# A hybrid decoder layer on one core: the first quarter of x and the first half slab by pairs of blocks

## The chip, the cores and the metric

One core of a Trainium2 chip runs the whole layer as one program. The metric is the time of one execution on the device in microseconds (us). Five engines work side by side: TensorE (PE, matmuls and transposes; its weight loads are shown as PEld), VectorE (DVE), ScalarE (ACT), GpSimd (POOL) and SyncE (SP, which here does little but issue DMAs). They meet only at semaphores.

## The reference

The layer takes x (256 tokens by 2048 features, float32) and one wide input projection, whose result is split over a state-space branch, latent attention and two gates; then an output projection, a layer norm, a SwiGLU feed-forward part and a second layer norm. Only the start of the input projection matters here:

```python
z = h @ w_in[l]                     # h = x (256, 2048)
u_ssm, c_q, c_kv, k_rope_raw, gate_logits = jnp.split(z, split_at, axis=-1)
```

## The kernel before, in words

All matmuls contract over features. A float32 operand is split in two parts that TensorE takes at full speed: a high part (a copy rounded by ScalarE) and a low part (VectorE: the value less its high part). A product of two blocks is then three matmuls: high by high, high by low, low by high.

**Weights** are packed on the host into slabs of 128 partitions by 1024 columns (8 blocks of 128 by 128, 512 KB). SP loads them into a ring of four buffers `raw`; ScalarE writes `whi` from them, VectorE `wlo`, TensorE multiplies. A load waits for the semaphore `lo_dve`, which counts finished low parts, since then its buffer is free. The first slabs (index `FRONT0 + n`) come in halves of 512 columns (`load_part`, `half_high`, `half_low`, `half_part`), so that work can begin sooner.

**x** is needed with features on the partitions. SP loads it in quarters of 512 columns, each as two loads for the two halves of the tokens (`load_x(q)`, semaphores `in_x[2q + t]`) into `xrow`. TensorE turns it by 128 by 128 transposes into PSUM (`turn_x`), one bank to a pair k of blocks (256 features): 4 transposes to a pair. ScalarE copies a bank's high part to `xT` (`x_high(k)`), VectorE its low part (`x_low(k)`).

**Order.** Everything is written by hand, one list for each engine, and each engine runs its own list in order. At the start SP issues two loads of x and two half slabs, and ScalarE itself issues the first half slab of the first slab (`load_part(ac, 0, 0)`), on a queue of its own. TensorE multiplies a zeroed tile eight times (`warm(8)`), waits for x, turns pairs 0 and 1 for each half of the tokens, multiplies the zeroed tile once more (`warm(1)`), and runs `first_part`: 12 matmuls of the first half slab by the first quarter of x (4 high by high, 4 of `wlo`, 4 by the low part of x), then `half_part(1, 0, 1)`, 12 more, then the turns of the next quarter. Each matmul there (a "product" below) has 256 columns.

The functions that the change touches, and what calls them, as the profile numbers them:

Of the kernel before, what the change touches and what calls it, by code (L numbers as in the profile page):

```python
# [21 lines left out]
P = 128  # L22
TOK = 256
# [22 lines left out]
FRONT0, FRONT_PER, FRONT_TURNS = 2, 4, 9  # L46
# [40 lines left out]
F32 = mybir.dt.float32  # L87
F32R = mybir.dt.float32r
I32 = mybir.dt.int32
ALU = mybir.AluOpType  # L90
ACT = mybir.ActivationFunctionType
# [39 lines left out]
def build(nc, slabs, x, pos, consts, cols, ssm, ssm_b, ssm_c, ln_rows, out):  # L131
    with ExitStack() as ctx:
        def sem(name):
            return ctx.enter_context(nc.semaphore(name))
# [17 lines left out]
        raw = at("raw", o, [P, RING, SLAB]); o += RING * SLAB * 4  # L152
        whi_at = o
        whi = at("whi", o, [P, RING, SLAB], F32R); o += RING * SLAB * 4
        wlo = at("wlo", o, [P, RING, SLAB], F32R); o += RING * SLAB * 4
# [35 lines left out]
        xrow = at("xrow", o, [P, 2, D]); o += 16384  # L191
# [10 lines left out]
        turn = at("turn", o, [P, 2, TOK])  # L202
# [45 lines left out]
        ps = ctx.enter_context(nc.psum_tensor("ps", [P, 8, 512], F32))  # L248
# [6 lines left out]
        ident = cst[:, C_ID:C_ID + P]  # L255
# [2 lines left out]
        raw_ready = [sem(f"raw_ready{s}") for s in range(RING)]  # L258
        hi_ready, lo_dve, slab_used = sem("hi_ready"), sem("lo_dve"), sem("slab_used")
        half_raw = [sem(f"half_raw{n}") for n in range(4)]  # L260
        half_hi, half_lo = sem("half_hi"), sem("half_lo")
        early_ready = [sem(f"early_ready{n}") for n in range(EARLY)]
        early_hi, early_lo, early_used = sem("early_hi"), sem("early_lo"), sem("early_used")
        h_shift, normed_act = sem("h_shift"), sem("normed_act")
# [3 lines left out]
        in_x = [sem(f"in_x{n}") for n in range(8)]  # L268
# [3 lines left out]
        xt_psum, xt_hi, xt_lo = sem("xt_psum"), sem("xt_hi"), sem("xt_lo")  # L272
# [53 lines left out]
        def load_part(eng, n, h):  # L326

            s, cut = (FRONT0 + n) % RING, slice(h * 512, h * 512 + 512)
            eng.dma_start(raw[:, s:s + 1, cut], slabs[FRONT_ORDER[n]:FRONT_ORDER[n] + 1, :, cut].rearrange("a p n -> p a n")
                          ).then_inc(half_raw[n] if h == 0 else raw_ready[s], 16)  # L330
# [5 lines left out]
        def _(sy):  # L336
# [15 lines left out]
            x_v = x.rearrange("(t p) d -> p t d", p=P)  # L352

            def load_x(q):
                for t in range(2):
                    sy.dma_start(xrow[:, t, q * 512:q * 512 + 512], x_v[:, t, q * 512:q * 512 + 512]
                                 ).then_inc(in_x[2 * q + t], 16)

            def load_half(n, h):
                load_part(sy, n, h)  # L360

            def front_load(v):
                load(FRONT_ORDER[v - FRONT0] if v < FRONT0 + 8 else v - FRONT0, v % RING, lo_dve, v - (RING - 1))
            load_x(0)
            load_half(1, 0)
            load_half(2, 0)
            load_x(1)
# [178 lines left out]
        def _(ac):  # L546
# [15 lines left out]
                nc.scalar.activation(whi[:, s, :], raw[:, s, :], ACT.Copy).then_inc(hi_ready, 1 + empty)  # L562


            load_part(ac, 0, 0)

            def x_high(k):
                ac.wait_ge(xt_psum, k + 1)
                nc.scalar.activation(xT[:, 2 * k:2 * k + 2, 0, :],
                                     ps[:, 2 + k % 5, :].rearrange("p (a t) -> p a t", a=2), ACT.Copy).then_inc(xt_hi, 1)  # L570

            def half_high(n, h):
                s, cut = (FRONT0 + n) % RING, slice(h * 512, h * 512 + 512)
                if h == 0:
                    ac.wait_ge(half_raw[n], 16)
                else:
                    ac.wait_ge(raw_ready[s], 16 if s >= FRONT0 else 32)
                nc.scalar.activation(whi[:, s, cut], raw[:, s, cut], ACT.Copy).then_inc(
                    half_hi if h == 0 else hi_ready, 1 + FRONT0 if (n, h) == (0, 1) else 1)

            half_high(0, 0)
            x_high(0)
            x_high(1)
            half_high(1, 0)
            half_high(2, 0)
# [333 lines left out]
            for k in range(4):  # L919
                high(0, DOWN0, 4, k + RING)  # L920
                half, cut = slice(64 * (k // 2), 64 * (k // 2) + 64), slice(1024 * (k % 2), 1024 * (k % 2) + 1024)
# [33 lines left out]
        def _(pe):  # L955
# [37 lines left out]
            def warm(n):  # L993

                for _ in range(n):
                    mm(ps[:, 1, 0:P], prob[:, 0:P], prob[:, 0:P], start=True, stop=True)

            def turn_x(q):
                for t in range(2):
                    pe.wait_ge(in_x[2 * q + t], 16)  # L1000
                    for k in (2 * q, 2 * q + 1):
                        if k >= 5:

                            pe.wait_ge(xt_lo, k - 4)
                        for a in range(2):
                            kt = 2 * k + a
                            ins = nc.tensor.transpose(ps[:, 2 + k % 5, a * TOK + t * P:a * TOK + (t + 1) * P],
                                                      xrow[:, t, kt * P:(kt + 1) * P], ident)
                        if t == 1:
                            ins.then_inc(xt_psum, 1)  # L1010

            def blocks(bank, w, s, b, kt0, n, a, first=False, last=False):

                for m in range(n):
                    ins = mm(ps[:, bank, 0:TOK], w[:, s, (b + m) * P:(b + m + 1) * P], xT[:, kt0 + m, a, :],  # L1015
                             start=(first and m == 0), stop=(last and m == n - 1))
                return ins

            def first_part():

                pe.wait_ge(half_hi, 1)
                for k in range(2):
                    pe.wait_ge(xt_hi, k + 1)
                    blocks(0, whi, FRONT0, 2 * k, 2 * k, 2, 0, first=(k == 0))
                pe.wait_ge(half_lo, 1)
                blocks(0, wlo, FRONT0, 0, 0, 4, 0)
                for k in range(2):
                    pe.wait_ge(xt_lo, k + 1)
                    blocks(0, whi, FRONT0, 2 * k, 2 * k, 2, 1)

            def half_part(n, h, bank):

                s, kt = (FRONT0 + n) % RING, 4 * h + (8 if n == 3 else 0)
                if h == 0:
                    pe.wait_ge(half_hi, n + 1)
                else:
                    pe.wait_ge(hi_ready, FRONT0 + n + 1)
                for k in range(2):
                    pe.wait_ge(xt_lo, kt // 2 + k + 1)
                    blocks(bank, whi, s, 4 * h + 2 * k, kt + 2 * k, 2, 0, first=(n < 3 and h == 0 and k == 0))  # L1040
                    blocks(bank, whi, s, 4 * h + 2 * k, kt + 2 * k, 2, 1)
                if h == 0:
                    pe.wait_ge(half_lo, n + 1)
                else:
                    pe.wait_ge(lo_dve, FRONT0 + n + 1)
                ins = blocks(bank, wlo, s, 4 * h, kt, 4, 0, last=(n == 3 and h == 1))
                if h == 1:
                    ins.then_inc(slab_used, 1 + FRONT0 if n == 0 else 1)
# [19 lines left out]
                    front_half(i, e, 1)  # L1068

            pe.wait_ge(warm_ready, 1)  # L1070
            warm(8)
            pe.wait_ge(ident_ready, 1)
            turn_x(0)
            warm(1)
            first_part()
            half_part(1, 0, 1)
            turn_x(1)
            half_part(2, 0, THIRD)
# [29 lines left out]
            for i in range(HG):  # L1108
# [182 lines left out]
                for h in range(2):  # L1291
                    head_low(i, 6 + h)
                    for t in range(2):
                        ins = row_tile(TP + t, (6 + h) % RING, t, cT, range(CT + 2 * h, CT + 2 * h + 2), h == 0, h == 1)
# [18 lines left out]
            for half in (0, 1):  # L1313
                for e in range(2):
# [3 lines left out]
                    for n in ((0, 1, 2, 3, 4, 5), (6, 7))[half]:  # L1318

                        pe.wait_ge(y_lo, n + 1)  # L1320
                        ins = fold_tile(e, e, n, yT, (n,), n == 0, n == UT - 1)
# [52 lines left out]
            for k in range(RING):  # L1374
                late_low(OUT0 + 24 + k)
                for t in range(2):
                    if k == 0:
                        row_bank(6 + t)
                    ins = out_part(k, t, first=(k == 0))
                ins.then_inc(slab_used, 1)  # L1380
            for k in range(RING, OUT_PER):
                late_low(OUT0 + 24 + k)
                ins = out_part(k, 0, last=(k == OUT_PER - 1))
# [3 lines left out]
            for k in (6, 7):  # L1387
                ins = out_part(k, 1, c1=256, last=(k == 7))
# [34 lines left out]
            for k in range(KT):  # L1423
# [8 lines left out]
                else:  # L1432
                    for e in range(2):
                        ins = early_block(k, e)
# [90 lines left out]
        def _(ve):  # L1525
            st = Steps(ve, dve_step)
            V = nc.vector
# [5 lines left out]
            def x_low(k):  # L1533
                ve.wait_ge(xt_hi, k + 1)
                V.tensor_tensor(xT[:, 2 * k:2 * k + 2, 1, :], ps[:, 2 + k % 5, :].rearrange("p (a t) -> p a t", a=2),
                                xT[:, 2 * k:2 * k + 2, 0, :].bitcast(F32), ALU.subtract).then_inc(xt_lo, 1)

            def half_low(n, h):
                s, cut = (FRONT0 + n) % RING, slice(h * 512, h * 512 + 512)
                if h == 0:  # L1540
                    ve.wait_ge(half_hi, n + 1)
                else:
                    ve.wait_ge(hi_ready, FRONT0 + n + 1)
                V.tensor_tensor(wlo[:, s, cut], raw[:, s, cut], whi[:, s, cut].bitcast(F32), ALU.subtract
                                ).then_inc(half_lo if h == 0 else lo_dve, 1 + FRONT0 if (n, h) == (0, 1) else 1)

            ve.wait_ge(index_ready, 1)
            V.tensor_scalar(ident, index[:], 0.0, None, ALU.is_equal).then_inc(ident_ready, 1)
            half_low(0, 0)
            x_low(0)  # L1550
            x_low(1)
            half_low(1, 0)
            half_low(2, 0)
# [808 lines left out]
```

## Time and profile before

| What | us |
|---|---|
| time, median of 3 runs (1322.74 to 1323.9) | 1323.16 |
| time of the profiled execution | 1323.33 |
| its span, from the first to the last instruction | 1321.3 |
| busy: TensorE | 1313.5 |
| busy: VectorE | 844.5 |
| busy: ScalarE | 650.8 |
| TensorE waiting ahead of its first product | 1.9 |

Times in the profile count from the span's start. A group of instructions in the timeline has its start, its length, the engine, the line in the program, the operation and the tiles it writes and reads, with xN for N records; a record is one pass of TensorE, and a matmul of two float32 tiles takes two. "Idle before" is the time in which the engine stood still ahead of it, with what ended that. A DMA's time to landing runs from its issue to its semaphore.

### The profile page before, as it was taken

The page shows a single profiled execution, that of the slowest core. Times are in us where ns is not written, and L with a number is a line of the kernel's source. Part 1 is how long each engine was busy: PE and PEld are TensorE (multiplying, and loading weights), DVE is VectorE, ACT ScalarE, POOL GpSimd, SP SyncE. Part 2 cuts the span into 40 slices and gives each one's busy share as a digit, 9 for nine tenths or more (in the row PEclk, how much of TensorE's full clock was granted, in tenths as well). Part 3 has the DMA queues.
Part 4 walks back from the last instruction along what each step waited for, and adds up shares of the span by engine and source line. Part 5 has one row for each costly group of instructions (what it writes and reads, how often), then busy time and mean ns, then how long its engine had stood idle before and what let it go on. Part 6 is the DMA issues. An engine that isn't in the chain of part 4 may idle for free.

```text
span 1321.3 us, 28135 instructions
## 1 busy us (share of the span) xinstructions
PE 1313.5 (99%) x10970; PEld 1241.9 (94%) x10970; DVE 844.5 (64%) x1263; ACT 650.8 (49%) x931; POOL 23.4 (2%) x52
## 2 busy tenths in 40 slices
PE   9999999999999999999999999999999999999998
PEld 9999999999999998889999999999999998888887
DVE  5887978787796776587565555555555546545545
ACT  5666557474656554365444444444444453334332
POOL 0022000000010000000000000000000000000000
PEclk9999999999999999999999999999999999999999
DMA  8666554554466776745666666666666676666572
GB/s 288 208 204 181 165 169 145 160 161 161 148 182 213 238 239 204 253 148 162 193 195 194 194 190 192 191 193 196 194 194 190 206 240 193 196 183 207 173 212 110
DMA packets 80782, 253.14 MB, mean 192 GB/s; under 512 B 16656, under 2 KB 17616, under 8 KB 80592
## 3 DMA queue, kind: packets, MB, share of 16 engines
q1 hardware_dynamic: 79024, 250.97, 60.2%
q8 instruction: 47, 0.77, 0.3%
q0 software_dynamic: 1408, 0.63, 0.2%
q10 hardware_dynamic: 288, 0.66, 0.1%
q14 instruction: 15, 0.12, 0.0%
HBM read 248.01 MB, written 2.10 MB: 189 GB/s over the span
## 4 chain that ended last, share of the span: by engine, by line
PE 95%; DVE 2%; DMA 2%; ACT 1%; issue 0%; SPq 0%; ACTq 0%; DVEq 0%
PE ps L975 21%; PE ps L977 21%; PE ps L976 21%; PE ps L987 9%; PE ps L988 9%; PE ps L989 9%; DMA raw<-slabs 1%; PE ps L1216 1%; DVE wlo L516 1%; PE ps L1015 1%; ACT whi L562 1%; PE ps L1212 1%; PE ps L1157 0%; DMA xrow<-x 0%; PE ps L1198 0%
## 5 line engine op out<-in xcount | busy, mean ns | idle before, releaser
L516 DVE TENSOR_TENSOR wlo<-raw,whi 128x1024 fp32r<-128x1024 f32 x444 | 540.0, 1224 | 335.2 <-ACT whi L562 333.2
L562 ACT ACTIVATE whi<-raw 128x1024 fp32r<-128x1024 f32 x444 | 470.4, 1061 | 503.3 <-PE ps L977 300.0
L975 PE MATMUL ps<-hT,whi 128*128 128x256 f32 x1376 | 378.4, 275 | 0.0
L976 PE MATMUL ps<-hT,whi 128*128 128x256 f32 x1376 | 378.4, 275 | 0.0
L977 PE MATMUL ps<-hT,wlo 128*128 128x256 f32 x1376 | 378.4, 275 | 0.0
L975 PEld LDWEIGHTS ps<-hT,whi 128*128 128x128 f32 x1376 | 258.3, 188 | 0.0
L976 PEld LDWEIGHTS ps<-hT,whi 128*128 128x128 f32 x1376 | 258.3, 188 | 0.0
L977 PEld LDWEIGHTS ps<-hT,wlo 128*128 128x128 f32 x1376 | 258.3, 188 | 0.0
L975 PE MATMUL ps<-xT,whi 128*128 128x256 f32 x720 | 203.2, 282 | 0.2 <-DVE wlo L516 0.2
L977 PE MATMUL ps<-xT,wlo 128*128 128x256 f32 x720 | 198.8, 276 | 0.0
L976 PE MATMUL ps<-xT,whi 128*128 128x256 f32 x720 | 198.7, 276 | 0.0
L975 PEld LDWEIGHTS ps<-xT,whi 128*128 128x128 f32 x720 | 135.3, 188 | 1.2 <-DVE wlo L516 0.4
L976 PEld LDWEIGHTS ps<-xT,whi 128*128 128x128 f32 x720 | 135.4, 188 | 0.1
L977 PEld LDWEIGHTS ps<-xT,wlo 128*128 128x128 f32 x720 | 135.2, 188 | 0.0
L989 PE MATMUL ps<-whi,act 128*128 128x512 f32 (+1 forms) x348 | 134.5, 387 | 0.0
L988 PE MATMUL ps<-wlo,act 128*128 128x512 f32 (+1 forms) x348 | 134.5, 387 | 0.0
L987 PE MATMUL ps<-whi,act 128*128 128x512 f32 (+1 forms) x348 | 134.5, 387 | 0.0
L989 PEld LDWEIGHTS ps<-whi,act 128*128 128x128 f32 x348 | 65.3, 188 | 13.4
L987 PEld LDWEIGHTS ps<-whi,act 128*128 128x128 f32 x348 | 65.3, 188 | 13.3
L988 PEld LDWEIGHTS ps<-wlo,act 128*128 128x128 f32 x348 | 65.3, 188 | 13.1
L975 PE MATMUL ps<-yT,whi 128*128 128x256 f32 x256 | 70.5, 276 | 0.0
L977 PE MATMUL ps<-yT,wlo 128*128 128x256 f32 x256 | 70.4, 275 | 0.0
(309 smaller groups left out, 1588.3 us busy)
## 6 DMA issues: line engine op xcount, KB each, us to landing
raw<-slabs SPq DMA_DIRECT2D x444, 512.0 KB, 3.7
xrow<-x SPq DMA_DIRECT2D x8, 256.0 KB, 6.0
rows<-x SPq DMA_DIRECT2D x4, 512.0 KB, 6.2
gb<-ln_rows SPq DMA_DIRECT2D x4, 512.0 KB, 7.8
eraw<-slabs SPq DMA_DIRECT2D x4, 512.0 KB, 6.6
gb<-ln_rows SPq DMA_DIRECT2D x1, 2048.0 KB, 7.8
raw<-slabs SPq DMA_DIRECT2D x7, 256.0 KB, 5.6
out<-rows SPq DMA_DIRECT2D x6, 256.0 KB, 2.3
```

The source lines that it names most:

```text
L516: unit.tensor_tensor(wlo[:, s, :], raw[:, s, :], whi[:, s, :].bitcast(F32), ALU.subtract).then_inc(done, 1)
L562: nc.scalar.activation(whi[:, s, :], raw[:, s, :], ACT.Copy).then_inc(hi_ready, 1 + empty)
L975: mm(ps[:, bank, 0:TOK], hi, src[:, kt, 0, :], start=(first and n == 0), stop=False)
L976: mm(ps[:, bank, 0:TOK], hi, src[:, kt, 1, :], start=False, stop=False)
L977: ins = mm(ps[:, bank, 0:TOK], lo, src[:, kt, 0, :], start=False, stop=(last and n == len(kts) - 1))
L987: mm(o_, xh, hi, start=(first and n == 0), stop=False)
L988: mm(o_, xh, lo, start=False, stop=False)
L989: ins = mm(o_, xl, hi, start=False, stop=(last and n == len(kts) - 1))
L1015: ins = mm(ps[:, bank, 0:TOK], w[:, s, (b + m) * P:(b + m + 1) * P], xT[:, kt0 + m, a, :], start=(first and m == 0), stop=(last and m == n ...
L1212: return mm(ps[:, SCORE[h], c0:c0 + n], qr[half_of(h % 2), h // 2, q * P:(q + 1) * P], zT[half_of(h % 2), 8 + h % 2, 0:n], start=start, st ...
L1216: return mm(ps[:, SCORE[h], c0:c0 + n], qT[:, h, q * P:(q + 1) * P], kT[:, h, 0:n], start=start, stop=stop)
```

## The change

Loads: the first quarter of x and the first half slab come by pairs of blocks, 256 columns each: x of pair 0 (both halves of the tokens in one load of 128 x 2 x 256), slab of pair 0, x of pair 1, slab of pair 1, all issued by SP. ScalarE issues no load at the start. ScalarE and VectorE split the slab in the same pieces, each ahead of the pair of x. TensorE turns pair 0, multiplies it by its two blocks of the slab (`first_high`: 2 products with `whi`, 2 with `wlo`), turns pair 1, multiplies likewise, and then does the 4 products by the low part of x (`first_low`). The zeroed tile is multiplied six times ahead of all and not in between.

```diff
+            def load_pair(k):
+                cut = slice(k * 256, k * 256 + 256)
+                sy.dma_start(xrow[:, :, cut], x_v[:, :, cut]).then_inc(in_x[k], 16)
+                sy.dma_start(raw[:, FRONT0:FRONT0 + 1, cut], slabs[0:1, :, cut].rearrange("a p n -> p a n")
+                             ).then_inc(pair_raw if k == 0 else half_raw[0], 16)
+
...
-            load_x(0)
+            load_pair(0)
+            load_pair(1)
...
-            load_part(ac, 0, 0)
-
...
-            half_high(0, 0)
+            def pair_high(k):
+                cut = slice(k * 256, k * 256 + 256)
+                ac.wait_ge(half_raw[0] if k else pair_raw, 16)
+                nc.scalar.activation(whi[:, FRONT0, cut], raw[:, FRONT0, cut], ACT.Copy).then_inc(pair_hi, 1)
+
+            pair_high(0)
             x_high(0)
+            pair_high(1)
             x_high(1)
...
-            def first_part():
-
-                pe.wait_ge(half_hi, 1)
-                for k in range(2):
-                    pe.wait_ge(xt_hi, k + 1)
-                    blocks(0, whi, FRONT0, 2 * k, 2 * k, 2, 0, first=(k == 0))
-                pe.wait_ge(half_lo, 1)
-                blocks(0, wlo, FRONT0, 0, 0, 4, 0)
-                for k in range(2):
-                    pe.wait_ge(xt_lo, k + 1)
-                    blocks(0, whi, FRONT0, 2 * k, 2 * k, 2, 1)
+            def first_high(k):
+
+                pe.wait_ge(pair_hi, k + 1)
+                pe.wait_ge(xt_hi, k + 1)
+                blocks(0, whi, FRONT0, 2 * k, 2 * k, 2, 0, first=(k == 0))
+                pe.wait_ge(pair_lo, k + 1)
+                blocks(0, wlo, FRONT0, 2 * k, 2 * k, 2, 0)
+
+            def first_low(k):
+
+                pe.wait_ge(xt_lo, k + 1)
+                blocks(0, whi, FRONT0, 2 * k, 2 * k, 2, 1)
...
-            warm(8)
+            warm(6)
             pe.wait_ge(ident_ready, 1)
-            turn_x(0)
-            warm(1)
-            first_part()
+            for k in range(2):
+                pe.wait_ge(in_x[k], 16)
+                for t in range(2):
+                    turn(k, t)
+                first_high(k)
+            first_low(0)
+            first_low(1)
             half_part(1, 0, 1)
```

`turn(k, t)` is the inner part of `turn_x` with nothing changed in it. VectorE's list changes as ScalarE's does (`pair_low(0)`, `x_low(0)`, `pair_low(1)`, `x_low(1)`).

TensorE's list before, from the start of the program (`prob` is the zeroed tile, `cst` holds the identity, `in_x` are the loads of x, `half_hi` and `half_lo` the parts of a half slab, `xt_hi` and `xt_lo` those of x):

```order
L996 MATMUL ps<-prob 128x128 [waits warm_ready]
L996 MATMUL ps<-prob 128x128 x7
L1007 MATMUL ps<-cst,xrow 128x128 [waits in_x0,ident_ready]
L1007 MATMUL ps<-cst,xrow 128x128 x3
L1007 MATMUL ps<-cst,xrow 128x128 [waits in_x1]
L1007 MATMUL ps<-cst,xrow 128x128 x3
L996 MATMUL ps<-prob 128x128
L1015 MATMUL ps<-xT,whi 128x256 [waits xt_hi,half_hi]
L1015 MATMUL ps<-xT,whi 128x256
L1015 MATMUL ps<-xT,whi 128x256 [waits xt_hi]
L1015 MATMUL ps<-xT,whi 128x256
L1015 MATMUL ps<-xT,wlo 128x256 [waits half_lo]
```

The same place with the change (`pair_hi`, `pair_lo` are the parts of a slab piece of 256 columns):

```order
L1009 MATMUL ps<-prob 128x128 [waits warm_ready]
L1009 MATMUL ps<-prob 128x128 x5
L1018 MATMUL ps<-cst,xrow 128x128 [waits in_x0,ident_ready]
L1018 MATMUL ps<-cst,xrow 128x128 x3
L1032 MATMUL ps<-xT,whi 128x256 [waits xt_hi,pair_hi]
L1032 MATMUL ps<-xT,whi 128x256
L1032 MATMUL ps<-xT,wlo 128x256 [waits pair_lo]
L1032 MATMUL ps<-xT,wlo 128x256
L1018 MATMUL ps<-cst,xrow 128x128 [waits in_x1]
L1018 MATMUL ps<-cst,xrow 128x128 x3
L1032 MATMUL ps<-xT,whi 128x256 [waits xt_hi,pair_hi]
L1032 MATMUL ps<-xT,whi 128x256
```

Four products now stand between the two groups of four transposes, and the second group waits in the list behind the copies of pair 0.

ScalarE's list before, from the start of the program:

```order
L329 DMA raw<-slabs 128x512
L578 ACT_TABLE_LOAD
L578 ACTIVATE whi<-raw 128x512 [waits half_raw0]
L569 ACTIVATE xT<-ps 128x2x256 [waits xt_psum] x2
L578 ACTIVATE whi<-raw 128x512 [waits half_raw1]
```

And with the change:

```order
L591 ACT_TABLE_LOAD
L591 ACTIVATE whi<-raw 128x256 [waits pair_raw]
L576 ACTIVATE xT<-ps 128x2x256 [waits xt_psum]
L591 ACTIVATE whi<-raw 128x256 [waits half_raw0]
L576 ACTIVATE xT<-ps 128x2x256 [waits xt_psum]
L585 ACTIVATE whi<-raw 128x512 [waits half_raw1]
```

The load has gone from this queue, and the second copy of x stands behind the second slab piece.

## Rows read from the trace of the kernel before

**Rows 1.** The page's first part: busy time of TensorE.

```profile
PE 1313.5 (99%) x10970; PEld 1241.9 (94%) x10970; DVE 844.5 (64%) x1263; ACT 650.8 (49%) x931; POOL 23.4 (2%) x52
```

**Rows 2.** Waits of PE, whole span: total, times, longest.

```profile
PE ps L996 <- POOL prob L521: 1.0, 1, 1.0
PE ps L1007 <- DMA xrow<-x: 0.6, 1, 0.6
...
PE ps L1015 <- ACT xT L569: 0.3, 1, 0.3
...
PE ps L975 <- DVE wlo L516: 0.2, 1, 0.2
```

**Rows 3.** The chain of waits in order of time: start, length, what.

```profile
1.19 4.81 DMA xrow<-x
...
6.04 0.45 PE ps L1007 x2
6.51 0.61 ACT xT L569
...
7.25 3.21 PE ps L1015 x24
```

**Rows 4.** Timeline of PE to 33 us.

```profile
1.00 3.78 PE L996 MATMUL ps<-prob 128*128 128x128 f32 x16 [1.00 <-POOL prob L521]
...
6.53 0.39 PE L996 MATMUL ps<-prob 128*128 128x128 f32 x2
...
10.31 1.03 PE L1007 MATMUL ps<-cst,xrow 128*128 128x128 f32 x8
...
30.06 1.98 PE L1015 MATMUL ps<-xT,whi 128*128 128x256 f32 x16
31.88 1.07 PE L1015 MATMUL ps<-xT,wlo 128*128 128x256 f32 x8
```

**Rows 5.** Timeline of ScalarE at the start.

```profile
4.99 0.63 ACT L578 ACTIVATE whi<-raw 128x512 fp32r<-128x512 f32 x1 [2.52 <-DMA raw<-slabs]
6.51 1.09 ACT L569 ACTIVATE xT<-ps 128x512 fp32r<-128x512 f32 x2 [0.89 <-PE ps L1007]
```

**Rows 6.** Issues on SP, and time to landing of single DMAs (issued 0.75, 0.75, 1.65, 3.08).

```profile
1.65 0.44 SPq L329 DMA_DIRECT2D raw<-slabs  x1
3.08 0.64 SPq L356 DMA_DIRECT2D xrow<-x  x1
...
xrow<-x SPq DMA_DIRECT2D x1, 256.0 KB, 3.9
raw<-slabs ACTq DMA_DIRECT2D x1, 256.0 KB, 4.2
...
raw<-slabs SPq DMA_DIRECT2D x1, 256.0 KB, 5.0
...
xrow<-x SPq DMA_DIRECT2D x1, 256.0 KB, 5.9
```

**Rows 7.** Windows: busy by engine, clock, DMA busy share, GB/s.

```profile
1.75:3.25 1.50, 1.50 (x9) 1.50 (x8) 0.07 (x1) 0.73 (x1) 0.00 (x0) 1.00 0.83 171
3.25:4.15 0.90, 0.90 (x7) 0.90 (x5) 0.00 (x0) 0.00 (x0) 0.00 (x0) 1.00 0.91 271
4.15:4.95 0.80, 0.79 (x5) 0.52 (x5) 0.00 (x0) 0.00 (x0) 0.00 (x0) 1.00 0.96 335
4.95:6.00 1.05, 0.48 (x4) 0.24 (x3) 0.34 (x1) 0.63 (x1) 0.00 (x0) 1.00 1.04 402
```

**Rows 8.** One line's instructions (20 to 60 us): copies of 256 columns, min/median/max ns.

```profile
L603 ACT ACTIVATE zT<-ps x8: 358/364/385, 22.1 to 55.8; 128x256 f32<-128x256 f32 x4, 128x256 f32 x4
```

**Rows 9.** Timeline of VectorE: low parts of the first two pairs.

```profile
7.14 1.29 DVE L1535 TENSOR_TENSOR xT<-ps,xT 128x512 fp32r<-128x512 f32 x2 [0.79 <-ACT xT L569]
```

**Rows 10.** Lines L996 (zeroed tile) and L1007 (transposes): ns, first and last start.

```profile
L996 PEld LDWEIGHTS ps<-prob x18: 190/333/333, 1.0 to 6.5; 128*128 128x128 f32 x18
...
L1007 PE MATMUL ps<-cst,xrow x32: 270/272/328, 4.8 to 18.8; 128*128 128x128 f32 x32
```

More of the change, by code:

```diff
@@ L260, in build @@
         half_raw = [sem(f"half_raw{n}") for n in range(4)]
+        pair_raw = sem("pair_raw")
         half_hi, half_lo = sem("half_hi"), sem("half_lo")
+        pair_hi, pair_lo = sem("pair_hi"), sem("pair_lo")
         early_ready = [sem(f"early_ready{n}") for n in range(EARLY)]
@@ L996, in warm, with turn @@
                     mm(ps[:, 1, 0:P], prob[:, 0:P], prob[:, 0:P], start=True, stop=True)
+            def turn(k, t):
+                if k >= 5:
+                    pe.wait_ge(xt_lo, k - 4)
+                for a in range(2):
+                    kt = 2 * k + a
+                    ins = nc.tensor.transpose(ps[:, 2 + k % 5, a * TOK + t * P:a * TOK + (t + 1) * P],
+                                              xrow[:, t, kt * P:(kt + 1) * P], ident)
+                if t == 1:
+                    ins.then_inc(xt_psum, 1)
             def turn_x(q):
@@ L1001, in turn_x @@
                     for k in (2 * q, 2 * q + 1):
[L1002 to L1010, printed above, removed]
+                        turn(k, t)
             def blocks(bank, w, s, b, kt0, n, a, first=False, last=False):
@@ L1034, in half_part @@
                 if h == 0:
-                    pe.wait_ge(half_hi, n + 1)
+                    pe.wait_ge(half_hi, n)
                 else:
@@ L1042, in half_part @@
                 if h == 0:
-                    pe.wait_ge(half_lo, n + 1)
+                    pe.wait_ge(half_lo, n)
                 else:
@@ L1070, in _ @@
             pe.wait_ge(warm_ready, 1)
-            warm(8)
+            warm(6)
             pe.wait_ge(ident_ready, 1)
-            turn_x(0)
-            warm(1)
-            first_part()
+            for k in range(2):
+                pe.wait_ge(in_x[k], 16)
+                for t in range(2):
+                    turn(k, t)
+                first_high(k)
+            first_low(0)
+            first_low(1)
             half_part(1, 0, 1)
@@ L1540, in half_low @@
                 if h == 0:
-                    ve.wait_ge(half_hi, n + 1)
+                    ve.wait_ge(half_hi, n)
                 else:
@@ L1548, in _, with pair_low @@
             V.tensor_scalar(ident, index[:], 0.0, None, ALU.is_equal).then_inc(ident_ready, 1)
-            half_low(0, 0)
+            def pair_low(k):
+                cut = slice(k * 256, k * 256 + 256)
+                ve.wait_ge(pair_hi, k + 1)
+                V.tensor_tensor(wlo[:, FRONT0, cut], raw[:, FRONT0, cut], whi[:, FRONT0, cut].bitcast(F32), ALU.subtract
+                                ).then_inc(pair_lo, 1)
+            pair_low(0)
             x_low(0)
+            pair_low(1)
             x_low(1)
```

## The prediction, made before the changed kernel was run

> **What bounds the kernel now.** I read the page's engine sums first: TensorE is busy for 1313.5 of 1321.3 us [rows 1], so only the stretches in which it does nothing useful can give anything back. The waits of PE say where those are [rows 2]: 1.0 us for the zeroed tile at the very start, 0.6 us for a piece of x, 0.3 us for the split of x, all before 7.3 us. Behind that PE runs without a visible wait as far as a single 0.2 us on a slab's low part, so a microsecond won in the front should travel to the end.
>
> The chain of waits at the front [rows 3] reads: the second load of x (issued at 1.19) lands at 6.00; PE turns it from 6.04; ScalarE copies from 6.51; PE multiplies from 7.25. The timeline of PE [rows 4] adds what is not useful: 16 records of warming (8 matmuls of the zeroed tile, two records each) from 1.00 to 4.78 and 2 more at 6.53. Before 7.25 PE has done 8 transposes of real work, about 1 us. Both copies of x end at 6.51 + 1.09 = 7.60 [rows 5]. PE then comes to the transposes of the next quarter at 10.31, which is 2.71 us behind 7.60. I take "PE reaches those transposes" as the mark by which both kernels are compared, since all orders are the same from there on.
>
> **The change, part by part.** *Warming.* 8 + 1 matmuls become 6. 3.78 / 16 = 0.236 us a record [rows 4], so six end at about 1.00 + 12 x 0.236 = 3.83. The two matmuls that go end ahead of 4.78, and the x of before landed at 0.75 + 3.9 = 4.65 [rows 6], so this is worth nothing by itself unless x comes earlier. The ninth (0.39 us at 6.53) lay under the copy of ScalarE: nothing too.
>
> *Loads.* The first quarter of x and the first half slab are 3 x 262 thousand bytes in both kernels, but were two loads of x on SP's queue beside one of the slab on ScalarE's, in rows of 2 KB; they become x, slab, x, slab on SP's queue, in rows of 1 KB, so 768 rows where there were 384. How long they take isn't in the trace and I bound it from two sides. By bytes: the windows [rows 7] give 171 x 1.5 = 256 thousand bytes moved by 3.25, 500 by 4.15, 768 by 4.95, 1190 by 6.00. Before, the first 524 were through at 4.22 and landed at 4.65 (x) and 0.75 + 4.2 = 4.95 (slab), 0.4 to 0.7 later; the first 786 were through at 4.99 and landed at 6.00, 1.0 later. The same curve gives: x of pair 0 (262) through at 3.3, landed at 3.9; slab of pair 0 (393) through at 3.75, landed at 4.4; x of pair 1 (655) at 4.6, landed at 5.5; slab of pair 1 (786) at 5.0, landed at 6.0. By rows: 402 / 2.05 = 196 rows a microsecond at full flow, less in the ramp (83% and 91% busy at 171 and 271 GB/s [rows 7], so there a row costs more than its bytes). If a row of 1 KB cost as much as one of 2 KB, the 384th would be through at 5.0 and the 768th at 6.9, landed at 5.7 and 8.0. The busy share near 1 at 402 GB/s looks like a limit by bytes, so I stand nearer to the first end and add 0.3 us to it. The Trainium skill, page DMA: Bandwidth & Descriptors, section Specifications, puts the least piece for full line rate at 512 B; by that the first end would hold and nothing be added. The ramp is not explained by that sentence.
>
> The loads behind are issued 0.9 us later (two more issues of 0.44 ahead [rows 6]), but the engines have a backlog by then, so this costs only if the queue runs dry: nothing. The second half slab landed at 1.65 + 5.0 = 6.65 [rows 6] and is wanted by ScalarE behind the copies, at 7.1 or later; cover 0.4 us. The next quarter of x landed at 3.08 + 5.9 = 9.0 and is wanted at 9.5 or later; cover 0.5 us. If those covers are gone, PE waits by the excess alone.
>
> *ScalarE and VectorE.* One copy of 512 columns (0.63) becomes two of 256, about 0.36 each by the copy of zT [rows 8]. ScalarE's order is now slab 0, x 0, slab 1, x 1, so each copy of x stands behind a slab piece that lands after its x. New waits: PE stands at the first products of pair 0 until ScalarE's copy, with the transposes of pair 1 queued behind; ScalarE stands at the second slab piece with the copy of x 1 queued behind, and VectorE and PE wait for that.
>
> *The new chain by bytes.* Slab 0 at 4.4; its copy 4.44 to 4.80; copy of x 0, 0.60, to 5.40; PE 0.14 later [rows 3] at 5.54: 4 products at 0.114 (16 take 31.88 - 30.06 = 1.82 [rows 4]) to 6.0; four transposes to 6.47 (6.04 to 6.51 before); copy of x 1 from 6.5 to 7.10. The other branch: slab 1 at 6.0, copied to 6.4, in time for the same 6.5. So the two branches meet, and the copy of x ends at 7.1 where it was 7.60: **0.5 us**. Behind it PE has 20 products to the mark where it had 22 left (two went between the copies before): 0.14 + 20 x 0.114 = 2.42 against 2.71, **0.3 us**. The low part of x 1 takes VectorE 0.65 to 0.7 (1.29 for two [rows 9]) and is ready about 0.8 behind the copy; PE wants it after 0.14 + 6 x 0.114 = 0.82: no wait. Sum by bytes: 0.8 us. With 0.3 us for the smaller rows: **0.5 us less**, with bounds +0.8 and, by rows, a loss: slab 1 at 8.0, copies to 9.0, mark at 11.4 instead of 10.31, **1.1 us more**.
>
> **Rivals.** *Late pieces.* Just that last case, or a part of it: one queue and twice the rows. For it: the busy ramp. Against it: full flow at 2 KB and the curve by bytes. It decides from a landing of slab 1 about 0.8 us later than 6.0. Gives 1323.3 to 1324.3.
>
> *The cold array.* This is the one that ends slower. The windows grant the full clock (1.00, the 2.4 GHz level) throughout [rows 7]. Yet a weight load of the zeroed tile takes 333 ns at the median and 190 at the least, which is one of the last two at 6.5 us, while the transposes last from 4.8 on what they last at 18.8 (270 to 328) [rows 10]: by its durations the engine ran slower, as at the 1.2 GHz level, through the unbroken 3.78 us of warming, and at full speed from about 4.8. The new order has an unbroken 2.83 us, then a gap till x lands, half a microsecond of transposes, a gap of about 1 us, and so on. If the rise comes only once the dense products run, everything on PE up to then takes up to double. Price: 8 transposes and 4 products on the chain, up to 1.0 us more; the 20 products (2.28 us) up to another 2.3, of which I take half: together 2.1 us against the gain of 0.5, so +1.6, with +0.6 and +2.8 as ends. It decides early: 24 products and 8 transposes are 32 x 0.114 = 3.6 us to the mark, and 5 of them at half speed cost 0.6, which is the gain. The Trainium skill, TensorE: Matmul & The Clock Gate, Part 1: The HAM clock gate, says that the array is cold by default, that sustained busy time and not a count of matmuls warms it, and Part 4: PE-mode transpose says that transposes don't count as busy in the same way; by these it would be this rival, as less unbroken busy time stands ahead of the products. The trace of before agrees on the slow start, and can't show what a gap does.
>
> *It does not do what it says:* x of pair 0 lands no sooner than 4.65, as the landing may be a fixed 4 us, and the gain by order is eaten by the two branches: 0 to 0.2 us, 1323.0 to 1323.2.
>
> **How the numbers follow.** The profiled execution took 1323.33 (span 1321.3, 2.03 outside it); the median of three is 1323.16, 0.17 lower, so the difference is set against the median: 1323.16 - 0.5 = 1322.7. Chances: forecast (gain 0.3 to 0.8) 0.50; no effect 0.15; late pieces 0.14; cold array 0.16; something behind the front that turns a shift into a larger difference, either way, 0.05. The three runs of before spread over 1.16 us, more than the whole forecast. A measurement of this kernel tells about 0.2%, 2.6 us, from no change; none of the cases but the far end of the cold array reaches that. Faster 0.02, same 0.94, slower 0.04. Range: the forecast's bound 1322.4 less half the spread gives 1321.9; above it takes in late pieces and most of the cold array, 1324.8.
>
> **What would show it.** Landing of the first x near 3.9 to 4.2 and of the last slab piece at 6.0 to 6.4; end of the second copy of x near 7.4; the transposes of the next quarter on PE at 9.6 to 10.0 instead of 10.31; from there all times earlier by the same amount, also the last store. Wrong if PE's products between the turns stand more than 0.2 us apart (cold array), if the last slab piece lands behind 6.9 (late pieces), or if the lead at the mark is there but has vanished by the slab whose low part PE waited 0.2 us for.

## The result, and the profile after

| | before | changed |
|---|---|---|
| median of 21 executions each, us | 1323.37 | 1325.88 |
| lowest to highest, us | 1322.44 to 1325.83 | 1322.21 to 1327.91 |
| span of the profiled execution, us | 1321.3 | 1324.1 |

The changed kernel is slower, by far less than 2%: the ratio on record is 1.0014, with a 95% interval of 1.0008 to 1.002. The medians lie 2.5 us apart, and the time lies above the range that was given. Its single times spread over 5.7 us, where those of before lie within 3.4: two of the 21 are below 1323 us, as four of before are, but 14 are over 1325 us, against two of before.

TensorE's timeline of the changed kernel answers to [rows 4] (L1009 is the zeroed tile, L1018 the transposes, L1032 the products):

```profile
1.01 2.93 PE L1009 MATMUL ps<-prob 128*128 128x128 f32 x12 [1.01 <-POOL prob L530]
3.87 1.05 PE L1018 MATMUL ps<-cst,xrow 128*128 128x128 f32 x4
5.70 0.47 PE L1032 MATMUL ps<-xT,whi 128*128 128x256 f32 x2 [0.78 <-ACT xT L576]
6.01 0.40 PE L1032 MATMUL ps<-xT,wlo 128*128 128x256 f32 x2
6.25 0.60 PE L1018 MATMUL ps<-cst,xrow 128*128 128x128 f32 x4
7.63 0.47 PE L1032 MATMUL ps<-xT,whi 128*128 128x256 f32 x2 [0.78 <-ACT xT L576]
7.94 0.43 PE L1032 MATMUL ps<-xT,wlo 128*128 128x256 f32 x2
8.18 2.75 PE L1032 MATMUL ps<-xT,whi 128*128 128x256 f32 x12
10.73 1.02 PE L1032 MATMUL ps<-xT,wlo 128*128 128x256 f32 x4
11.58 0.60 PE L1018 MATMUL ps<-cst,xrow 128*128 128x128 f32 x4
```

Up to 8.2 us all goes about as planned: the first product starts at 5.70 instead of 7.25, the second group at 7.63. Ahead of each of the two PE stands still for 0.78 us, for a copy of ScalarE. Then 12 products take 10.73 - 8.18 = 2.55 us, 0.21 each, where a product took 0.114 [rows 4]. The next quarter is turned at 11.58, not at 10.31; this point is the mark by which the prediction compares the kernels. The windows of the same kernel (busy time by engine, granted clock, DMA share, GB/s) show where the level changes:

```profile
5.00:6.00 1.00, 0.30 (x2) 0.33 (x3) 0.41 (x1) 0.56 (x1) 0.00 (x0) 1.00 0.77 229
6.00:7.00 1.00, 0.85 (x8) 0.61 (x6) 0.43 (x2) 0.53 (x2) 0.00 (x0) 1.00 0.99 377
7.00:8.00 1.00, 0.37 (x3) 0.40 (x4) 0.76 (x2) 1.00 (x3) 0.00 (x0) 1.00 0.97 277
8.00:9.00 1.00, 1.00 (x7) 1.00 (x7) 1.00 (x3) 0.58 (x2) 0.00 (x0) 0.58 1.00 356
...
11.00:12.00 1.00, 1.00 (x8) 1.00 (x8) 0.00 (x0) 0.00 (x0) 0.00 (x0) 0.71 1.05 404
12.00:13.00 1.00, 1.00 (x11) 1.00 (x10) 0.00 (x0) 0.56 (x2) 0.00 (x0) 1.00 1.04 397
```

The granted clock is 0.50, the 1.2 GHz level, from 8.2 to 11.6 us, although PE is busy in all of it. What stands ahead of the fall is three microseconds in which PE was busy for 0.30, 0.85 and 0.37. The 16 products in these 3.4 us would have taken 1.8 at 0.114 each, so some 1.6 us are lost; the mark is 1.27 later than before, so the new order has given back 0.3. In the column of before there was no stretch below 1.00 ahead of its last microseconds.

The span is 2.8 us longer, so 1.5 us of it lie behind the mark. A part of these is in the waits of PE for low parts of slabs, which [rows 2] has once with 0.2 us (total, times, longest):

```profile
PE ps L988 <- DVE wlo L525: 0.8, 3, 0.3
```

All three fall between 444 and 476 us; the one of before falls between 60 and 80. Theory A says: the clock in the front is the cause. Its rival B says: the new order of loads does harm behind the front, and these waits are its mark. A third, C, which goes with A: these waits are chance of one execution.

### The profile page after: what moved, and what is told of

The parts are those of the page before. It is cut to its first block, busy times and chain, and to the rows that moved or that the text cites. A ratio compares the mean times of both kernels' runs of the same rounds, so it can differ in the third digit from the quotient of the medians.

```text
span 1324.1 us, 28127 instructions
## 1 busy us (share of the span) xinstructions
PE 1315.3 (99%) x10964; PEld 1243.1 (94%) x10964; DVE 844.4 (64%) x1264; ACT 650.8 (49%) x932; POOL 23.5 (2%) x52
## 4 chain that ended last, share of the span: by engine, by line
PE 95%; DMA 2%; DVE 2%; issue 1%; ACT 1%; DVEq 0%; ACTq 0%; SPq 0%; POOL 0%; POOLq 0%
PE ps L988 21%; PE ps L989 21%; PE ps L990 21%; PE ps L1000 9%; PE ps L1001 9%; PE ps L1002 9%; PE ps L1032 2%; DMA raw<-slabs 2%; PE ps L1238 1%; DVE wlo L525 1%; PE ps L1234 1%; PE ps L1179 0%; PE ps L1220 0%; PE ps L1193 0%; PE ps L1201 0%
```

## The experiments

Twelve runs were made, on three chips (the runs whose names begin with e, g and h); "before" is the kernel before, run beside them. Two of the twelve are the changed kernel itself (g1, h4), one is the kernel before (g4), and h2 is e1 again. The column of turns is the mark.

| run | median us | over 1325 us | ratio to before (95%) | turns of next quarter at, us | span, us |
|---|---|---|---|---|---|
| e1_fill | 1322.84 | 0 of 11 | 0.9999 (0.999 to 1.0008) | 10.07 | 1320.3 |
| e2_warm8 | 1323.5 | 2 of 11 | 1.0006 (0.9997 to 1.0015) | 10.47 | 1321.4 |
| e3_turns_first | 1324.08 | 2 of 11 | 1.0005 (0.9996 to 1.0014) | 11.03 | 1322.3 |
| e4_before_warm6 | 1324.75 | 3 of 11 | 1.0011 (1.0002 to 1.002) | 12.28 | 1322.7 |
| g1_after_again | 1323.66 | 4 of 11 | 1.0007 (0.9998 to 1.0016) | 10.08 | 1321.3 |
| g2_fill1 | 1323.81 | 1 of 11 | 1.0001 (0.9992 to 1.001) | 9.94 | 1321.7 |
| g3_two_queues | 1324.83 | 4 of 11 | 1.0006 (0.9997 to 1.0015) | 12.35 | 1323.6 |
| g4_before_again | 1322.8 | 0 of 1 | one execution | 10.55 | 1321.0 |
| h1_no_warm | 1325.91 | 9 of 11 | 1.0018 (1.0009 to 1.0027) | 12.87 | 1325.2 |
| h2_fill_again | 1322.84 | 0 of 11 | 0.9998 (0.9988 to 1.0007) | 10.08 | 1320.7 |
| h3_before_fill | 1323.27 | 1 of 11 | 1.0002 (0.9993 to 1.0011) | 10.47 | 1322.5 |
| h4_after_third | 1325.25 | 6 of 11 | 1.0011 (1.0001 to 1.002) | 12.97 | 1324.4 |

Before, beside these: 1323.27 (33 executions, one over 1325) for e, 1323.27 (27, none) for g, 1323.38 (33, none) for h. Only for e4, h1 and h4 does the interval lie above 1; the others can't be told from before.

**The gaps filled (e1_fill, h2_fill_again).**

```diff
                 for t in range(2):
                     turn(k, t)
+                warm(3)
                 first_high(k)
```

> The changed kernel with three multiplications of the zeroed tile in each of the two gaps of PE (between the four transposes of a pair and its first product). Theory A (PE stands still for 0.8 us twice between 4.9 and 7.6 us, the granted clock then falls to 0.50 at 8.2 and stays there to 11.6, which costs 1.7 us): the clock stays 1.00, the 20 products behind the second copy take 2.3 us instead of 3.95, the next quarter is turned at 9.9 to 10.0, and the time is 0.3 to 0.6 us below that of the kernel before, over 2 us below the changed one. Theory B (the time is lost behind the front, by the new order of loads; 1.0 us of it shows in waits for low parts between 425 and 475 us): the front is as fast as A says or not, but the time stays at least 1 us above that of before.

```profile
3.91 1.02 PE L1018 MATMUL ps<-cst,xrow 128*128 128x128 f32 x4
4.76 0.83 PE L1009 MATMUL ps<-prob 128*128 128x128 f32 x6
5.70 0.47 PE L1032 MATMUL ps<-xT,whi 128*128 128x256 f32 x2
...
8.23 1.54 PE L1032 MATMUL ps<-xT,whi 128*128 128x256 f32 x12
9.61 0.62 PE L1032 MATMUL ps<-xT,wlo 128*128 128x256 f32 x4
10.07 1.03 PE L1018 MATMUL ps<-cst,xrow 128*128 128x128 f32 x8
```

This is the timeline of PE in e1_fill. The filling ends just as the copy is there (5.70, as in the changed kernel), so it costs nothing, and the 12 products take 9.61 - 8.23 = 1.38 us instead of 2.55. The order of the loads is that of the changed kernel, and the loss is gone: this refutes B, as far as a loss of 1 us or more goes. The changed kernel did not run on this chip. The second time:

> The changed kernel with three multiplications in each gap, once more, for the size of its lead: theory A expects 0.3 to 0.6 us below before, no fall of the clock, few times over 1324, and 1 to 2 us below the changed kernel run beside it.

It came out alike: 1322.84 again, and in the two runs together no execution of 22 is over 1325 us, where the changed kernel has 24 of 43 (14 of 21, 4 and 6 of 11). It lies 2.4 us below the changed kernel run beside it (h4), a little more than the 1 to 2 us that were expected.

**The warming (e2_warm8, e4_before_warm6, h1_no_warm).** e2 puts `warm(8)` for `warm(6)` in the changed kernel.

> The changed kernel with eight multiplications of the zeroed tile at the start instead of six. Theory A with the gaps as the cause: the rise comes in the first stretch in both, so two more there do not help; x waits until 4.7, everything to the first product is 0.7 us later, the fall of the clock remains; time equal to the changed kernel or up to 0.7 us more. Theory A2 (the shortened warming is the cause, not the gaps): no fall of the clock, mark at 10.3 to 10.6, time equal to before. Theory B: clock apart, the time stays 1 us or more above before.

The profile shows no fall, though the gaps of 0.78 us are still there twice; turns at 10.47. The median, 1323.5, is 0.2 us above before, and 2 of 11 are over 1325. It came out nearer to "the warming counts" than to "only the gaps count", but its interval reaches 0.15% above before, and the changed kernel did not run beside it. e4 shortens the warming of the kernel before and changes nothing else:

```diff
-            warm(8)
+            warm(6)
             pe.wait_ge(ident_ready, 1)
             turn_x(0)
-            warm(1)
             first_part()
```

> The kernel before, with six multiplications of the zeroed tile at the start and none between the transposes and the first product; nothing else changed. Theory A: PE then does only 0.9 us of transposes between 3.8 and 7.25, so its clock falls too (or has not risen), at 8 to 12 us, and the time is 1.2 to 2.5 us above before. Theory B: the loads are those of before, so no loss: within 0.3 us of before.

```profile
1.00 2.93 PE L996 MATMUL ps<-prob 128*128 128x128 f32 x12 [1.00 <-POOL prob L521]
5.12 1.98 PE L1007 MATMUL ps<-cst,xrow 128*128 128x128 f32 x8 [1.19 <-DMA xrow<-x]
7.46 1.20 PE L1015 MATMUL ps<-xT,whi 128*128 128x256 f32 x4 [0.35 <-ACT xT L569]
8.45 1.05 PE L1015 MATMUL ps<-xT,wlo 128*128 128x256 f32 x4
9.30 2.67 PE L1015 MATMUL ps<-xT,whi 128*128 128x256 f32 x12
```

Here PE stops at 3.9, waits 1.19 us for x, and everything up to the end of the 12 products at 11.8 is slow: 2.51 us for them. So three matmuls of a zeroed tile, none of them on the chain of waits, carried 1.5 us in the median of the kernel before (interval 0.3 to 2.6). Loads and order are untouched here, so a loss of this kind needs nothing of B. Which of the three counts is not separated. h1 leaves out all warming of the changed kernel:

> The changed kernel with no multiplication of the zeroed tile at all. Theory A: this sets the price of a cold front for certain. PE does nothing until x lands at 3.75, so it is at the low level for all 32 operations to the next quarter's turns and for some us behind; mark at 12 to 13.5 us in every execution, times of 1325 to 1327 with hardly any near 1322.5. If the level of the clock did not matter (theory B), nothing would change, as the warming ended just as x landed: time as the changed kernel's, below 1324 on this chip.

```profile
9.58 2.76 PE L1032 MATMUL ps<-xT,whi 128*128 128x256 f32 x12
```

Turns at 12.87, median 1325.91, none of 11 below 1324.7. This is the price of a front at the low level throughout, 2.5 us, and the times over 1325 of the changed kernel are of this size.

**The changed kernel again (g1_after_again, h4_after_third), and before again (g4_before_again).**

> The changed kernel itself, once more. Theory A (the loss is the clock in the front, which depends on where an execution meets the chip's clock control): a profile shows products behind the second copy at half speed for some 3 us or, if this execution was lucky, none; the median stays 1 to 2.5 us over before, and the single times lie in two groups, one near 1322.5 and one near 1326. Theory B (waits for low parts between 444 and 476 us, 1.0 us, belong to the change): they show again, in this profile too. Theory C (those waits are chance of one execution): they are gone, and the end is later than before by what the front lost, less 0.4 us.

> The changed kernel a third time. Theory A: median between 1323.5 and 1326, the share of times over 1325 between a third and nearly all; the profile has either products at the usual spacing and a mark near 10.1, or a stretch at half speed and a mark of 11.5 or later, nothing between 10.6 and 11.2. Theory C: waits for low parts, if there are any, at other places than in the two profiles before.

The two runs are the same program. Timeline of PE, g1_after_again:

```profile
3.90 1.09 PE L1018 MATMUL ps<-cst,xrow 128*128 128x128 f32 x4
5.77 0.47 PE L1032 MATMUL ps<-xT,whi 128*128 128x256 f32 x2 [0.78 <-ACT xT L576]
...
8.24 1.55 PE L1032 MATMUL ps<-xT,whi 128*128 128x256 f32 x12
9.63 0.62 PE L1032 MATMUL ps<-xT,wlo 128*128 128x256 f32 x4
10.08 1.03 PE L1018 MATMUL ps<-cst,xrow 128*128 128x128 f32 x8
```

And h4_after_third:

```profile
3.88 1.08 PE L1018 MATMUL ps<-cst,xrow 128*128 128x128 f32 x4
5.74 0.77 PE L1032 MATMUL ps<-xT,whi 128*128 128x256 f32 x2 [0.78 <-ACT xT L576]
...
8.57 0.77 PE L1032 MATMUL ps<-xT,whi 128*128 128x256 f32 x2 [0.78 <-ACT xT L576]
...
9.56 2.76 PE L1032 MATMUL ps<-xT,whi 128*128 128x256 f32 x12
12.12 1.05 PE L1032 MATMUL ps<-xT,wlo 128*128 128x256 f32 x4
12.97 1.45 PE L1018 MATMUL ps<-cst,xrow 128*128 128x128 f32 x8
```

Up to 5.7 us they agree within 0.03. Then the first two products take 0.47 in one and 0.77 in the other: in g1 the engine came up to full speed between 4.9 and 5.8, in h4 it did not, and did not before 13 us. From there h4 goes as h1 does, which has no warming at all: 12 products from 9.56 and 9.58, the mark at 12.97 and 12.87. With the first profile there are three courses of one program: risen and kept (10.08, span 1321.3), risen and fallen (11.58, span 1324.1), not risen (12.97, span 1324.4). That is 2.8 to 3.1 us in the span for 1.5 to 2.9 at the mark. Nothing in the program differs. The waits for low parts are 0.8 us at 444 to 476 in the first profile, 0.2 between 60 and 80 us in g1, absent in h4. Elsewhere they are 0.7 in e3 and 0.6 in h1, both between 60 and 80, and 0.4 in g2 between 480 and 500. The first profile of before has 0.2 between 60 and 80 too, the second none. So the waits of 444 to 476 us do not come back in the same program, and the place at 60 to 80 is one that before has as well: neither is a mark of the new loads. That they are chance, and not helped by the change a little, isn't shown by so few profiles.

Not all that g1 was expected to show came: its median is 0.4 us over before, not 1 to 2.5, and its interval (0.9998 to 1.0016) takes in no difference. The executions over 1325 are there, 4 of 11 against none of 27 beside them. What was expected of h4 came.

> The kernel before, a second profile. All theories: clock 1.00 throughout, transposes of the next quarter at about 10.3 us, time 1322.4 to 1324. Theory C would allow single waits of some tenths of a us at another place than in the first profile.

```profile
5.04 2.10 PE L1007 MATMUL ps<-cst,xrow 128*128 128x128 f32 x8 [0.25 <-DMA xrow<-x]
```

1322.8 us, turns at 10.55, no waits for low parts at all. But the weight loads of these 8 transposes take 218 ns in the mean, where those of the first profile take 142: here before too is at the low level until some 6.8 us, and ScalarE's first copy of x starts at 6.77 instead of 6.51 [rows 5]. That fits the difference of 0.24 us in the mark. With all nine warmings the engine comes up either ahead of 4.8 or behind 6.7, but in both profiles ahead of the first product.

**Turns before products (e3_turns_first).** The changed loads, with `first_high(0)` and `first_high(1)` behind both turns:

> The changed loads and copies, but PE turns both pairs before any product, as before the change. PE's work up to the mark is the same, and so nearly is the sum of its idle time (one long gap ahead of x of pair 1, one ahead of the second copy). Theory A (it is the little work between 5 and 8 us that counts): the clock falls as in the changed kernel, time within 0.5 us of it. Theory A3 (the order turn, product, turn, product is what breaks it): clock at 1.00 and time 0 to 0.5 us below before. Theory B: over before by 1 us, clock at 1.00.

The profile shows neither a recorded fall nor full speed: PE waits 0.89 us for x of pair 1 and its first products at 6.66 take 0.78 for two, as in h4; full speed comes during the 12 products. Mark 11.03, median 1324.08. So in this execution six warmings left PE slow with the turns ahead of the products as well; A3, which wanted a time below before, gets no support. The interval (0.9996 to 1.0014) takes in before and a loss of 1.8 us, so between A's two numbers it is inconclusive. B's "clock at 1.00" is in the column, but not in the durations.

**One in each gap (g2_fill1).**

> As the run with three multiplications of the zeroed tile in each gap of PE, but one in each: PE still stands still for about 0.5 us twice. Theory A: between the two, some executions fall and some do not; median 1323.0 to 1325.0. If the length of the gaps does not matter but only that they are there, as the changed kernel (1325 to 1326); if a third of the filling suffices, as three (1322.8).

1323.81, one of 11 over 1325, the profile at full speed. The share over 1325 lies between those of none (4 of 11 on this chip) and of three (0 of 22 on the others), as A has it; the median does not, as none has 1323.66 here. By 11 executions the two can't be told apart.

**The slab pieces on ScalarE's queue (g3_two_queues).**

```diff
+            for k in range(2):
+                cut = slice(k * 256, k * 256 + 256)
+                ac.dma_start(raw[:, FRONT0:FRONT0 + 1, cut], slabs[0:1, :, cut].rearrange("a p n -> p a n")
+                             ).then_inc(pair_raw if k == 0 else half_raw[0], 16)
```

> The kernel with three multiplications in each gap, but the two slab pieces of pairs 0 and 1 are loaded from ScalarE's queue instead of SP's. If the single queue holds the pieces back (the transfer engines were busy for only 0.50 of 4.15 to 4.95 us in the changed kernel, and the last piece landed at 6.4 instead of 6.0): the last piece lands at 5.6 to 6.0, the second copy of x ends 0.3 to 0.5 us sooner, the time is 0.3 to 0.5 us below the one-queue version with three. If the transfers are bound by bytes or rows in all: no change within 0.2 us.

Time to landing of the pieces, x issued at 0.75 and 1.24, slab at 0.76 and 1.22:

```profile
xrow<-x SPq DMA_DIRECT2D x1, 256.0 KB, 3.8
raw<-slabs ACTq DMA_DIRECT2D x1, 128.0 KB, 3.3
...
xrow<-x SPq DMA_DIRECT2D x1, 256.0 KB, 4.4
raw<-slabs ACTq DMA_DIRECT2D x1, 128.0 KB, 3.7
```

The same in the changed kernel, issued at 0.75, 1.75 (x), 1.25 and 2.22 (slab):

```profile
xrow<-x SPq DMA_DIRECT2D x1, 256.0 KB, 3.0
...
xrow<-x SPq DMA_DIRECT2D x1, 256.0 KB, 4.2
raw<-slabs SPq DMA_DIRECT2D x1, 128.0 KB, 2.8
...
raw<-slabs SPq DMA_DIRECT2D x1, 128.0 KB, 4.2
```

With two queues the last slab piece lands at 4.9 instead of 6.4, and x of pair 1 at 5.6 instead of 5.95, but x of pair 0 at 4.55 instead of 3.75. The first part of the expectation holds and more; the second copy of x, though, ends at 9.4 instead of 7.5. The time went the other way, to 1324.83, though five of the 11 are below 1323.8 and the interval (0.9997 to 1.0015) takes in before. The profile is of one of the slower executions, 1325.7:

```profile
4.67 1.09 PE L1021 MATMUL ps<-cst,xrow 128*128 128x128 f32 x4 [0.74 <-DMA xrow<-x]
5.55 1.49 PE L1012 MATMUL ps<-prob 128*128 128x128 f32 x6
```

Warming ends at 3.9, x comes at 4.6, and behind this gap the engine is still at the low level: the filling takes 1.49 us where it took 0.83 in e1, and ends 0.15 us after the products could have started. Products are slow until about 10.2; turns at 12.35. So in this execution the better landing was lost to the clock, although both gaps behind the turns were filled. That the new gap at 3.9 to 4.7 is what did it is argued from one profile and not shown.

**The gaps of the kernel before, filled (h3_before_fill).** `warm(2)` between the turns of the two halves of the tokens, `warm(3)` instead of `warm(1)` ahead of the first product:

> The kernel before, with its own gaps filled: two multiplications between the turns of the two halves of the tokens, three instead of one ahead of the first product. If the lead of the filled changed kernel came from the filling alone, this one has it too (0.3 us or more below before). If it came from the order by pairs (turns of the next quarter at 10.07 against 10.31), this one equals before within 0.2 us and the filled changed kernel lies 0.2 to 0.4 us below it.

1323.27 against 1323.38 for before: nothing. The filling alone brings no lead that 11 executions show.

## Why the prediction was wrong, step by step

*Where it was right.* Landings were forecast at 3.9 (x 0), 4.4 (slab 0), 5.5 (x 1), 6.0 (slab 1) with 0.3 added; they are 3.75, 4.05, 5.95, 6.42. The end of the second copy was forecast at 7.4 and is 6.89 + 0.60 = 7.49:

```profile
4.06 0.42 ACT L591 ACTIVATE whi<-raw 128x256 fp32r<-128x256 f32 x1 [2.02 <-DMA raw<-slabs]
4.96 0.60 ACT L576 ACTIVATE xT<-ps 128x512 fp32r<-128x512 f32 x1 [0.48 <-PE ps L1018]
6.40 0.42 ACT L591 ACTIVATE whi<-raw 128x256 fp32r<-128x256 f32 x1 [0.84 <-DMA raw<-slabs]
6.89 0.60 ACT L576 ACTIVATE xT<-ps 128x512 fp32r<-128x512 f32 x1
```

These are ScalarE's instructions of the changed kernel, against [rows 5]. In an execution at full speed the mark is at 10.08, 0.23 sooner than in the first profile of before and 0.47 sooner than in the second, where the forecast had 0.3 to 0.7. The mark of before moves by 0.24 itself, which one profile couldn't tell. The late pieces did not happen (the last landed at 6.42, and 6.9 was their sign), x of pair 0 did land sooner than 4.65, and PE has no wait for a load in the changed kernel's front, so no cover was used up.

*A small miss.* The curve of bytes was carried over from before, but the transfer engines were not as busy:

```profile
4.15:4.95 0.80, 0.77 (x4) 0.40 (x2) 0.42 (x1) 0.33 (x1) 0.00 (x0) 1.00 0.50 122
4.95:6.00 1.05, 0.30 (x2) 0.33 (x3) 0.41 (x1) 0.60 (x1) 0.00 (x0) 1.00 0.77 226
```

That is the changed kernel in two windows of [rows 7], which had 0.96 and 335, 1.04 and 402. With a second queue (g3) the first of them had 0.99 and 337. The landings by bytes were 5.5 and 6.0 for x 1 and slab 1, and they came 0.45 and 0.42 us later; the 0.3 that was added took in most of it. Whether the one queue or the later issues (1.75 and 2.22 instead of 1.24 and 1.22) made the engines idle, no run separates.

*The step that failed* is the first one, on warming: "worth nothing by itself" and "nothing too". The two matmuls at 3.83 to 4.78 and the one at 6.53 were costed by the chain of waits, where they are not. They have a work of their own: e4 takes just these three from the kernel before and loses 1.5 us, as its products then run at 0.21 us each instead of 0.114. With the same six warmings e1 fills the gaps and has no loss. So what failed is a term put at nothing, on the ground that nothing waits for it, while the terms behind it (0.114 us to a product) counted on a level that it helped to reach. The rows for it were at hand and were used for the rival only: the weight loads of the zeroed tile take 333 ns up to the end of the first stretch and 190 at 6.4 us [rows 10], so the engine came up no sooner than about the end of those two matmuls. The margin was small, and the second profile of before (g4), in which it came up only behind 6.7, shows how small.

*The rival was the right one, with too small a chance and too small a size.* The cold array had 0.16. The changed kernel is over 1325 in 24 of 43 executions, before in 3 of 114, so it is the likelier case; the shares of the three chips (14 of 21, 4 of 11, 6 of 11) can't be told apart by so few. Its price was put at +1.6 with +0.6 and +2.8 as ends, because I took half of the 20 products at low speed; in the profiles it is 2.8 and 3.1 us in the span, and 2.5 in the median on record, inside those ends. All 20 products ran slowly when the engine did not rise, and 16 of them when it fell. The form was partly missed too: I looked for a late rise, and the profile on record shows a rise that is taken back. So its sign, products between the turns more than 0.2 us apart, is there in h4 (0.21 to 0.29) and not in the profile on record, where those products were fast and the ones behind them slow. The form of PE's work between 4 and 6 us was described rightly ("half a microsecond of transposes, a gap of about 1 us"). The Trainium skill (TensorE: Matmul & The Clock Gate, Part 1: The HAM clock gate) says that sustained busy time warms the array and not a count of matmuls, and that the point of the rise shifts from run to run. On the second the runs agree: one program rose before 5.8 us in one execution and after 13 in another. The first is not tested apart, as no run here changes the count without the time. The sentence of the Trainium skill that transposes do not count as busy in the same way (Part 4: PE-mode transpose) isn't tested by any run here either.

*What would have kept the range.* With cases this far apart and neither excluded by a row, the upper end had to take in the whole price, 2.3 for all products and 1.0 on the chain, less 0.5: 1326, which the 1325.88 measured would just have met.

*What stays open.* Whether the filled version beats before: both runs put it at 1322.84, about 0.4 to 0.5 us below (1323.27 and 1323.38), which fits the mark, but the intervals reach from 0.1% below before to 0.07 and 0.08% above. And how much of the span behind the front is chance: from the mark to the end it is 1310.2 to 1312.5 us in the profiles at hand, 1311.0 and 1310.5 for before, and the profile on record is the highest. Of its 2.8 us only 1.3 are explained by the clock in the front; 0.8 lie in waits for low parts (0.2 in before), and the rest has no cause here. The medians rest on more: a front at the low level throughout (h1) costs 2.5 us in the median and 2.3 to 2.6 at the mark.

## What to carry to other kernels

A matmul that feeds nothing can still be at work: before shortening a warming or opening a gap near the start, look at the durations of TensorE's records on either side, and ask at which level the next dense stretch will run. A gain of some tenths of a microsecond bought by making TensorE wait in short pieces should be paired with filling for those pieces, sized from the wait in the trace (three matmuls for 0.78 us here). The filling is no guarantee: in the profile of g3 it ran at the low level, took 1.49 us and reached into the products' time. A gap ahead of it may be why, which isn't shown. And where single times of a kernel fall in two groups, take two or three profiles of the same program: they say more than one profile of each of two programs.

## What the runs showed that I had not expected

- The granted clock of the profile says 1.00 up to the first change that it records. In h4_after_third it says 1.00 throughout the front, while its products take 0.21 us each up to 12.9 us. These are the lines of that kernel between 9.5 and 12.5 us and of g1_after_again between 8.2 and 10 (busy, mean ns):

```profile
L1032 PE MATMUL ps<-xT,whi 128*128 128x256 f32 x12 | 2.8, 415 | 0.0
```

```profile
L1032 PE MATMUL ps<-xT,whi 128*128 128x256 f32 x12 | 1.5, 277 | 0.0
```

  Only the duration tells the level there.
- The clock fell at 8.2 us, half a microsecond into dense work and behind three microseconds with the two gaps in them, and stayed down to 11.6 with PE fully busy.
- Two queues brought the last of four pieces 1.5 us sooner and the first 0.8 us later, with the same bytes.
